# Adding expert outputs into DRAM rows by an accumulating scatter, in a hybrid mixer and mixture-of-experts kernel

## What is computed

```python
def hierarchical_moe(h, ...):                 # h: 512 x 1024, 4 groups of 4 experts
    gl = t @ w_group + b_group                # one group per token
    ...
    top_v, top_i = lax.top_k(el_sel, 2)       # two experts in that group
    wts = jax.nn.softmax(top_v, axis=-1) * g_prob[:, None]
    ...
    for e in range(16):
        a = jax.nn.silu(t @ w_gate[e]) * (t @ w_up[e])      # 1024 x 512 each
        out = out + gate[:, e:e + 1] * (a @ w_down[e])      # 512 x 1024
    return out

    x = x + hierarchical_moe(rmsnorm(x, norm_ffn), ...)
    return rmsnorm(x, norm_final)
```

## Time and profile before

| | |
|---|---|
| Median of 3 runs | 778.89 us (778.33 to 779.47) |
| The profiled execution's own time | 779.35 us |
| Its span in the trace | 777.6 us |
| Busy: TensorE, VectorE, ScalarE, GpSimd | 718.8, 511.1, 409.1, 121.1 us |
| The chain that ended last | TensorE 86%, VectorE 7%, issue 3%, ScalarE 2%, DMA 1%, GpSimd 1% |
| DMA, both directions | 155.46 MB, mean 200 GB/s |
| Indirect gathers of x, issue to landing | median 8.2 us, 16 of them |
| Indirect scatters of y, issue to landing | median 7.4 us, 16 of them |

### The profile page before, as it was taken

One profiled execution on the slowest core, in us unless ns is written; L12 is line 12 of the kernel. 1 busy time (PEld: TensorE's weight loads), 2 busy tenths in 40 slices (PEclk: granted clock), 3 DMA queues, 4 the chain that ended last, 5 costly groups with the idle time before them and its releaser, 6 DMA issues.

```text
span 777.6 us, 10199 instructions
## 1 busy us (share of the span) xinstructions
PE 718.8 (92%) x3595; PEld 602.4 (77%) x3595; DVE 511.1 (66%) x554; ACT 409.1 (53%) x415; POOL 121.1 (16%) x111
## 2 busy tenths in 40 slices
PE   4999997999999999999999989999999999999820
PEld 3898986888888888888888848888888888888720
DVE  5778653465623417070544777999999999999818
ACT  6626655366432223131324416777778787777602
POOL 5000000000000000000000040333444443333210
PEclk9999998999999999999999998999999999999965
DMA  8552330000033232333575359999999999999044
GB/s 282 169 154 56 108 109 0 1 1 28 15 97 126 89 108 60 102 94 121 183 270 212 121 185 385 395 397 373 373 367 380 373 379 376 376 379 364 38 160 191
DMA packets 85312, 155.46 MB, mean 200 GB/s; under 512 B 6373, under 2 KB 37215, under 8 KB 84772
## 3 DMA queue, kind: packets, MB, share of 16 engines
q1 hardware_dynamic: 78452, 137.39, 49.6%
q0 software_dynamic: 6832, 17.69, 6.0%
HBM read 151.17 MB, written 12.58 MB: 211 GB/s over the span
## 4 chain that ended last, share of the span: by engine, by line
PE 86%; DVE 7%; issue 3%; ACT 2%; DMA 1%; POOL 1%; POOLq 0%; DVEq 0%; ACTq 0%
PE ps L461 26%; PE ps L463 26%; PE ps L462 26%; PE ps L1419 2%; PE ps L1199 1%; PE ps L1201 1%; PE ps L1345 1%; PE ps L1445 1%; DMA xe<-h_rows,x_col 1%; DMA y_in<-y_rows 1%; DVE x L2019 1%; PE ps L1373 1%; DVE x L2026 1%; PE ps L1114 0%; PE ps L1331 0%
## 5 line engine op out<-in xcount | busy, mean ns | idle before, releaser
L444 DVE TENSOR_TENSOR ring_lo<-raw_a,ring_hi 128x2048 fp32r<-128x2048 f32 (+2 forms) x58 | 115.6, 1995 | 97.1 <-ACT ring_hi L438 96.4
L444 DVE TENSOR_TENSOR ring_lo<-raw,ring_hi 128x2048 fp32r<-128x2048 f32 x71 | 161.1, 2291 | 13.8 <-ACT ring_hi L438 12.4
L438 ACT ACTIVATE ring_hi<-raw 128x2048 fp32r<-128x2048 f32 x71 | 136.3, 1920 | 20.3 <-PE ps L463 20.3
L461 PE MATMUL ps<-hT_hi,ring_hi 128*128 128x512 f32 x288 | 113.9, 396 | 4.3 <-DVE v_lo L1568 2.3
L438 ACT ACTIVATE ring_hi<-raw_a 128x2048 fp32r<-128x2048 f32 (+2 forms) x58 | 97.5, 1680 | 32.2 <-PE ps L463 32.2
L463 PE MATMUL ps<-hT_hi,ring_lo 128*128 128x512 f32 x288 | 112.8, 392 | 0.0
L462 PE MATMUL ps<-hT_lo,ring_hi 128*128 128x512 f32 x288 | 112.7, 391 | 0.0
L461 PE MATMUL ps<-ring_hi,xT_hi 128*128 128x512 f32 x240 | 95.9, 399 | 0.6 <-DVE xT_lo L1902 0.6
L463 PE MATMUL ps<-ring_hi,xT_lo 128*128 128x512 f32 x240 | 94.6, 394 | 0.0
L462 PE MATMUL ps<-ring_lo,xT_hi 128*128 128x512 f32 x240 | 94.5, 394 | 0.0
L461 PEld LDWEIGHTS ps<-hT_hi,ring_hi 128*128 128x128 f32 x288 | 54.4, 189 | 16.8 <-DVE v_lo L1568 2.4
(11 more groups left out here) (344 smaller groups left out, 1285.9 us busy)
## 6 DMA issues: line engine op xcount, KB each, us to landing
raw<-in_w_down SPq DMA_DIRECT2D x25, 1024.0 KB
raw<-in_w_gate SPq DMA_DIRECT2D x47, 512.0 KB
raw<-in_w_up SPq DMA_DIRECT2D x47, 512.0 KB
raw_a<-in_w_in SPq DMA_DIRECT2D x15, 1024.0 KB
raw_a<-in_w_gate SPq DMA_DIRECT2D x17, 512.0 KB
raw_a<-in_w_up SPq DMA_DIRECT2D x17, 512.0 KB
raw_a<-in_w_down SPq DMA_DIRECT2D x7, 1024.0 KB
raw_a<-in_w_in SPq DMA_DIRECT2D x10, 512.0 KB, 7.6
```

Of the source, the lines that this page charges most:

```text
L438: act.activation(ring_hi[:, c[0] % SPLIT, 0:width], buf[:, 0:width], ACT.Copy).then_inc(hi_ready, 1)
L444: dve.tensor_tensor(ring_lo[:, s, 0:width], buf[:, 0:width], ring_hi[:, s, 0:width].bitcast(F32), ALU.subtract).then_inc(lo_ready, 1)
L461: pe.matmul(out_ap, l_hi, r_hi, start=start, stop=False, skip_group_check=True)
```

## The change

Five things are done.

1. The weighted sum moves. `y_rows` is gone. x2, the input of the experts' sum, is written to a DRAM buffer `acc_rows` with one row per token (GpSimd, four DMAs of 512 KB, three beside the rows of h and one after two x gathers). `y_half` multiplies by a weight per row, `w_col`, and the scatter adds its rows to `acc_rows` (`compute_op=ALU.add`). It is issued only after the scatter before it has landed.
2. The weights per row come by a route of their own: `wts` goes to DRAM (`w_rows`), and for each tile GpSimd copies the column of row numbers and gathers 128 rows of 4 bytes (`w_load`). `ye_free`, for which `y_half` waits, now also says that the weights of that tile are there. The column of token numbers for the scatter (`t_load`) is set ahead of the waits for y.
3. At the end SyncE reads `acc_rows` back into x2 (four DMAs of 512 KB), and only norm, scaling and store are left; the combinations are gone.
4. Steps 13 and 14 of the expert loop (those that finish experts 14 and 15) are written out. The last `a_transpose` stands between the two chunks of `down` of expert 15, with buffers of its own (`aT_hi_end`, `aT_lo_end`), and the gather, transposes and evacuations of a 17th tile, which only overflow needs, go into the overflow part.
5. The overflow loop of seven turns stands under one condition on each engine.

In the core of the diff below the first pieces are GpSimd's, then come SyncE's reads, ScalarE's and VectorE's `y_half`, and VectorE's last steps (ScalarE's have the same order) and end.

```diff
             for t in range(TB):
                 pool.wait_ge(h2_ready, t + 1)
                 pool.dma_start(h2_rows[t * P:(t + 1) * P, :], h2[:, t, :]).then_inc(h2_out, 16)
+                if t < TB - 1:
+                    pool.wait_ge(x2_ready, t + 1)
+                    pool.dma_start(acc_rows[t * P:(t + 1) * P, :], x2[:, t, :]).then_inc(acc_in, 16)
...
-            def y_store(tile, b, before):
-
+            def w_load(tile, b):
+
+                pool.tensor_copy(y_col[b][:, :], y_row[:, bass.ds(tile, 1)]).then_inc(y_col_set, 1)
+                pool.wait_ge(y_col_set, tile + 1)
+                pool.sem_inc(pool_free, 1)
+                pool.indirect_dma_start(w_col[b][:, :], None, w_rows[:, :],
+                                        bass.IndirectOffsetOnAxis(y_col[b][:, :].bitcast(U32), 0),
+                                        bounds_check=2 * S - 1, oob_is_err=False).then_inc(w_in_col[b], 16)
...
+            def y_store(tile, b, earlier, following):
+
+                t_load(tile, b)
+                if earlier is not None:
+                    pool.wait_ge(y_out[1 - b], 16 * earlier)
+                    pool.sem_inc(pool_free, 1)
+                    pool.wait_ge(w_in_col[1 - b], 16 * (earlier + 1))
+                    pool.sem_inc(ye_free, 1)
                 pool.wait_ge(y_a, tile + 1)
                 pool.wait_ge(y_v, tile + 1)
                 pool.sem_inc(pool_free, 1)
-                pool.tensor_copy(y_col[b][:, :], y_row[:, bass.ds(tile, 1)]).then_inc(y_col_set, 1)
-                pool.wait_ge(y_col_set, tile + 1)
-                pool.sem_inc(pool_free, 1)
-                pool.indirect_dma_start(y_rows[:, :], bass.IndirectOffsetOnAxis(y_col[b][:, :].bitcast(U32), 0),
-                                        ye[b][:, :], None, bounds_check=2 * S - 1, oob_is_err=False).then_inc(y_out[b], 16)
-                if before is not None:
-                    pool.wait_ge(y_out[1 - b], 16 * before)
-                    pool.sem_inc(ye_free, 1)
+                pool.indirect_dma_start(acc_rows[:, :], bass.IndirectOffsetOnAxis(t_col[b][:, :].bitcast(U32), 0),
+                                        ye[b][:, :], None, bounds_check=S - 1, oob_is_err=False,
+                                        compute_op=ALU.add).then_inc(y_out[b], 16)
+                if following is not None:
+                    w_load(following, b)
...
-            for t in range(TB):
-                pool.dma_start(y_in[:, t, :, :], y_rows[2 * t * P:2 * (t + 1) * P, :].rearrange("(p r) d -> p r d", r=2)) \
-                    .then_inc(y_back[t], 16)
+            pool.sem_inc(acc_done, 1)
...
+            sp.wait_ge(acc_done, 1)
+            for t in range(TB):
+                sp.dma_start(x2[:, t, :], acc_rows[t * P:(t + 1) * P, :]).then_inc(acc_back[t], 16)
...
-                act.activation(ye[b][:, 0:512], bank(5), ACT.Copy).then_inc(y_a, 1)
+                act.activation(ye[b][:, 0:512], bank(5), ACT.Copy, scale=w_col[b][:, :]).then_inc(y_a, 1)
...
-                dve.tensor_copy(ye[b][:, 512:1024], bank(6)).then_inc(y_v, 1)
+                dve.tensor_scalar(ye[b][:, 512:1024], bank(6), w_col[b][:, :], None, ALU.mult).then_inc(y_v, 1)
...
+            for step in (NE - 4, NE - 3):
+                c0 = C_MOE + 10 + PER_E * step
+                for i in range(PER_E):
+                    if step == NE - 3 and i == PER_E - 1:
+                        aT_l(NE, aT_lo_end, aT_hi_end)
+                    split_lo(dve, K(c0 + i + 2))
...
             y_half(K(C_OVER - 3), 0, NE - 1)
-            aT_l(NE)
             y_half(K(C_OVER - 1), 1, NE)
...
-            for t in range(TB + 1):
-                if t < TB:
-                    dve.wait_ge(y_back[t], 16)
-                    link(dve.scalar_tensor_tensor(x2[:, t, :], y_in[:, t, 0, :], wts[:, 0, t:t + 1], x2[:, t, :],
-                                                  ALU.mult, ALU.add))
-                    dve.scalar_tensor_tensor(x2[:, t, :], y_in[:, t, 1, :], wts[:, 1, t:t + 1], x2[:, t, :],
-                                             ALU.mult, ALU.add).then_inc(comb_ready, 1)
...
```

More of the change, by code:

```diff
@@ L87, in stage_map @@
     o = base
-    for name, size in (("const", 9984), ("ring_hi", 4 * CW * SPLIT), ("ring_lo", 4 * CW * SPLIT),
+    for name, size in (("const", 10048), ("ring_hi", 4 * CW * SPLIT), ("ring_lo", 4 * CW * SPLIT),
                        ("raw", 4 * CW * RAW), ("m", 98304), ("t", 30720)):
@@ L163, in build_trunk @@
     y_col = [sb(f"y_col{b}", [P, 1], I32, "const") for b in range(2)]
+    t_col = [sb(f"t_col{b}", [P, 1], I32, "const") for b in range(2)]
+    w_col = [sb(f"w_col{b}", [P, 1], F32, "const") for b in range(2)]
     lgs = sb("lgs", [P, TB, NG + NE], F32, "const")
@@ L389, in build_trunk @@
         ye_free = sem("ye_free")
-        y_back = [sem(f"y_back{t}") for t in range(TB)]
-        comb_ready = sem("comb_ready")
+        acc_back = [sem(f"acc_back{t}") for t in range(TB)]
         res_ready = sem("res_ready")
@@ L662, in _ @@
             pool.sem_inc(consts_ready, 1)
-            pool.sem_inc(ye_free, 2)
             for g in range(4):
@@ L994, in _ @@
                     xe_hi(3)
-            with act.Fori(0, NE // 2 - 1) as j:
+            with act.Fori(0, NE // 2 - 2) as j:
                 for n in range(2):
@@ L1446, in a_transpose, with down @@
                 ins.then_inc(at_ps, 1)
-            def down(n, c0, j, read, per=RAW_MOE):
+            def down(n, c0, j, read, per=RAW_MOE, between=None, hi=aT_hi, lo=aT_lo):
                 pe.wait_ge(at_l, n)
@@ L1458, in down @@
                             o = kk * 1024 + half * 512
-                            ins = three(pe, bank(5 + half), aT_hi[:, f * P:(f + 1) * P], aT_lo[:, f * P:(f + 1) * P],
+                            ins = three(pe, bank(5 + half), hi[:, f * P:(f + 1) * P], lo[:, f * P:(f + 1) * P],
                                         wh[:, o:o + 512], wl[:, o:o + 512], f == 0, f == 3)
                     ins.then_inc(chunk_used, 1)
+                    if i == 0 and between is not None:
+                        between()
             for i in range(4):
@@ L1999, in _ @@
                             xe_lo(step + 4)
+            for step in (NE - 4, NE - 3):
+                c0 = C_MOE + 10 + PER_E * step
+                for i in range(PER_E):
+                    if step == NE - 3 and i == PER_E - 1:
+                        aT_l(NE, aT_lo_end, aT_hi_end)
+                    split_lo(dve, K(c0 + i + 2))
+                    if i == 0:
+                        y_half(K(c0 - 1), step % 2, step + 1)
+                    if i == 1:
+                        aT_l(step + 2)
+                    if i == 3:
+                        gated(step + 3)
+                        if step == NE - 4:
+                            xe_lo(NE)
```

194 lines of the change are left out of this document (125 added, 69 removed).

## The result

The changed kernel is slower. Its median is 786.28 us (785.03 to 787.93, 4 runs) against 779.16 (778.33 to 779.47, 4 runs), a ratio of 1.0095, 95% interval 1.0077 to 1.0114. The forecast was 778.2, no change to speak of; the time lies in the range, the direction was missed. Its profiled execution took 785.03 us with a span of 783.3, so 5.7 us more span than before; the median shows 7.1, since that execution has the lowest time of the four.

The account below looks back on a forecast made before the run. TensorE was taken as the bound at 17.7 us per expert, VectorE and the weight stream close behind. Tail -11.2, last two experts -0.3 and accumulating scatter +10.8 gave -0.7 on the 778.89 median: 778.2 us, range 767 to 790.

Parts of the forecast that it names:

- The loaded half of the DMA engines: Gathers and scatters: an expert's 64 rows fall on one half of the engines, 1.33 us of each per tile.
- the lead: Weight stream ahead of ScalarE's splits: 12.7 us at chunk 18, 7.5 at chunk 78, 8.5 left at the last chunk.
- The price of the addition: Accumulating scatter: reading the x2 rows costs one more pass, 1.33 us per tile on the loaded half; +10.8 us in all.
- Free read: Rival for the accumulating scatter: the read hides in the write and costs near 0, total 767.4 us; chance 0.20.
- three passes: Rival for the accumulating scatter: reads and write don't overlap, 2.66 us more per tile, total 796.9; dearer than 1.5: chance 0.28.
- By bytes: Rival for the accumulating scatter: 0.26 MB more per tile at 382 GB/s, 0.7 us, total about 769.5; chance 0.08.
- 13e + 1.3 - 8.5: Last chunk: thirteen scatters at e (addition's time per tile) plus last x2 tile, less 8.5 us lead; 10.1 remain.
- The start: Before the first experts: 1.3 us for the last x2 tile, nothing for the weights' trip through DRAM, perhaps 3 once.
- The tail: After the last y half: earlier scatter -1.05, shorter read-back -2.2, no combinations -7.95 us; together -11.2 before the addition.
- The last two experts: Moved last transposes and dropped 17th tile: TensorE resumes at 736.45 for 736.75, -0.3 us; bound -2.4.
- the rival in which it really goes: TensorE's 2.4 us wait for aT_lo before the last down really vanishes, taking 2 us from any case; no chance given.
- The scaling at eviction: y half: multiplication replaces a 0.69 us copy; counted as nothing, perhaps 0.1 us per tile, hidden by VectorE's spare 1.1.

Follow-up runs that it names:

- the start cleaned: Changed kernel with the last x2 tile written with the others and the weights' route left out (rows added unweighted): 779.97 us, ratio 1.0015 to the kernel before.
- the last kernel: Changed kernel with rows spread over both halves, last x2 tile written early, expert 15's y half ahead of VectorE's last low split: 767.98 us, ratio 0.9853.

## Why the prediction failed, point by point

**The bound and the mechanism were right.** The loaded half of the DMA engines, one more pass of it per tile, the lead eaten up and the splits then bound to the stream: each was found as described, only sooner (from chunk 35 of 96 on, the seventh expert's gate and up, not in the second half of the experts). Chunk 82 came at 692.85, just over the 685 to 692 given.

**The price of the addition was nearly right.** From chunk 22 to 91 the changed kernel needs 224.8 us for 210.55, 14.25 over twelve scatters: 1.19 each, with the start cleaned (225.6 - 210.55) / 12 = 1.25, against 1.33. Of the 1.19 the addition itself is 1.1. The other 0.1 has no cause shown: without the weights' route the stretch is no shorter (224.9).

The estimate that the prediction drew from the Trainium skill ("Collectives: The Full Stack", section "The bandwidth ceiling: the fold count and why AG ≠ RS ≠ AR", two source reads on one ring) was 1.24. The measured 1.1 to 1.25 agree with it, but can hardly tell it from 1.33.

"Free read" fell, and so did "three passes" (2.66). "By bytes" (0.7) fell for this kernel and comes close for the one with spread rows (0.7 to 0.9).

**The step that failed is the lead.** The formula was 13e + 1.3 - 8.5, a delay at the last chunk less the lead there. The prediction had itself read 7.5 us at chunk 78, less than the 8.5 that it subtracted. The lead isn't spent at the end of the stream alone. In the kernel before it is 5.4 us at chunk 87 and rises to 8.5 at chunk 95, since the last chunks are loaded at up to 418 GB/s for 382, and SyncE issues the last two without waiting for a landing. After chunk 90 no chunk was late in the changed kernel either. The largest delay counts, over all chunks: delay of the stream at that chunk less the lead at that chunk. The rows for it were in the trace of before. That was worth 3.1 us; the clean start shows it in a run of its own, and the waits of the kernel with the plain scatter agree.

**The start was mis-sized.** 1.3 us were counted for the last x2 tile and none for the weights' store; the two cost 5.3 together, 3.3 each if alone. The prediction looked whether the weights arrive in time for the first y half (they did: nobody waited for them) and not what their store does to the stream beside it. That was worth 4.0 us.

At chunk 87 the sum reads: 5.3 + 14.25 - 5.4 = 14.2. The thirteenth scatter adds 1.2 until chunks 89 and 90, whose splits come 15.4 us later than before. Between chunks 91 and 92, when no chunk is late any more, 0.7 go again: ScalarE waits 0.6 us for TensorE's transposes there, where it waited 1.25 before. That is about the 0.6 that the prediction took off. The dropped 17th tile isn't the cause, for in the kernel before with parts 4 and 5 alone chunk 95 is no nearer to the old time than chunk 91 (0.84 and 0.85 late). After chunk 95 0.35 more go: 14.3, where 9.2 was forecast.

**The tail** was forecast at -9.9 with the addition in it and gave -8.6. With the plain scatter it is 21.4 us for 32.8, -11.4, where -11.2 was worked out. That the two are so close is in part luck. The scatter begins 0.87 and not 0.15 us after the y half (+0.7), and the read-back takes 3.25 for 3.0 (+0.25). But from the scatter to the read-back a plain one takes 3.74 us for the 4.27 kept (-0.5), and from the first square to the end of the last scaling it is 10.4 for 11.1 (-0.7): the first tile takes 3.7 and not the whole 4.4, the others 2.22 as said. What is left is the addition, 2.9 us dearer there and not 1.33 (+1.6). These make the 1.3.

**The last two experts** brought nothing clear of noise for the 0.3 forecast. The named wait went from `aT_lo` to the y half, as said, and the rival in which it really goes fell. The scaling at eviction takes 745 ns on VectorE and 673 on ScalarE, 0.06 and 0.1 us more than the copies, and was covered.

By the same account the sum -0.7 becomes +14.3 - 8.6 = +5.7. Lead and start together were short by 7.1 us and the tail by 1.3. The price of the addition beside the stream, counted 1.85 too high (17.3 for 14.25 + 1.2), hid some of it. That the time still fell into 767 to 790 is owed to that and to a range made wide for a dearer addition, so it is luck in part. The chance of slower, 0.38, rested on the price of the addition alone; a late start and the place of the lead were no rivals. One small slip: with e = 1.5 the prediction's formula gives 780.6 and not 780.4.

## What to carry to other kernels

Read the slack of a stream at every chunk and take the smallest, chunk by chunk against the delay expected there. A partly filled tile whose rows stand together may load only half of the DMA engines: spreading the rows is an edit of two lines and was worth 17 us here, but only in the kernel in which the stream was the bound; where TensorE was, it was worth nothing. Ask of every new small transfer what it does to the large ones beside it, not only when it lands.

## What the runs showed of the hardware

*Tiny pieces slow a stream out of proportion.* A store of 4 KB in 512 pieces of 8 bytes took 10.1 us to land beside the weights and cost them 1.8 us behind the late x2 tile, 3.3 without it. Twice the pieces, in two stores at once, cost no more in time (785.81 us for 786.28). Why is open; larger pieces weren't tried.

*An accumulating scatter alone on the engines* is dearer than one beside the stream. Stretches of the changed kernel and, last, of the kernel before around the last scatter:

```profile
761.00:766.00 5.00, 0.00 (x0) 0.00 (x0) 0.00 (x0) 0.00 (x0) 0.57 (x1) 0.65 0.38 57
...
746.50:749.50 3.00, 0.00 (x0) 0.00 (x0) 0.00 (x0) 1.28 (x1) 0.49 (x1) 0.65 0.24 94
```

0.38 x 5 x 16 = 30 engine-us for 285 KB, against 0.24 x 3 x 16 = 11.5 for 282 KB. By engine time that is 2.6 times a plain one, but the stream beside it was delayed by no more than one pass (1.1 to 1.25 us). Why the two differ is open; no run shows it.

*A wait of 2.9 us, and the clock after it.* TensorE's last `down` of the changed kernel, behind its wait:

```profile
751.01:753.01 2.00, 2.00 (x7) 1.63 (x8) 0.00 (x0) 0.00 (x0) 1.39 (x2) 0.82 0.00 0
753.01:755.80 2.79, 2.79 (x8) 2.21 (x7) 0.00 (x0) 0.00 (x0) 1.69 (x4) 0.52 0.41 53
```

The granted clock falls to 0.52, near the lower of its two levels (1.2 and 2.4 GHz), after TensorE stood idle for 2.9 us and resumed. In the chain of waits (start, us, what) one matmul takes 0.43 us there and 0.23 behind it:

```profile
752.81 0.43 PE ps L471
...
756.27 0.23 PE ps L471
```

After the wait of 1.1 us in the last kernel the matmuls stay at 0.39 to 0.40 us each and the granted clock at 1.00. From TensorE's restart to the start of the last y half that kernel needs 735.58 to 741.34, 5.8 us. The changed kernel with rows spread, which has the wait of 2.9 us, needs 735.49 to 744.01, 8.5 us, at 0.50 for most of it:

```profile
735.49 0.77 PE L471 MATMUL ps<-ring_hi,aT_hi_end 128*128 128x512 f32 x1 [2.95 <-DVE ye L2054]
...
736.00:741.00 5.00, 5.00 (x13) 3.93 (x12) 0.00 (x0) 0.00 (x0) 3.08 (x4) 0.50 0.36 49
```

So behind the shorter wait the slow matmuls are saved as well, here 2.7 us.
